# Products of b_o and gates1 between the steps of a recurrence, and a head norm spread over the next job

## The reference

```python
def mlstm_chunkwise(...):                 # branch 1, 4 heads of 128, chunks of 128 tokens
    def step(carry, xs):                  # run forwards and backwards over the 6 chunks
        ...
        w = jnp.exp(dmat - m_t[..., None])
        wqk = w * jnp.einsum('bthd,bshd->bhts', qc, kc)
        num = einsum(wqk, vc) + a[..., None] * einsum(c_prev, qc)
        h = num / jnp.maximum(jnp.abs(den), jnp.exp(-m_t))[..., None]
        ...
        c_new = decay[..., None, None] * c_prev + einsum(ws, vc, kc)
y_b = sigmoid(o_pre) * (h_forward + h_backward)        # o_pre is the product called b_o

def merge_branches(ys, gate_logits, w_branch, w_out):
    g = sigmoid(gate_logits)                           # the products gates0 to gates3
    merged = sum(g[:, :, i] * (y @ w_branch[i]) for i, y in enumerate(ys))
    return merged @ w_out
```

## Time and profile before

| | |
|---|---|
| median of 3 runs | 3787.38 us (3786.98 to 3789.18) |
| the profiled execution, its own time | 3781.9 us |
| its span, first to last instruction | 3780.2 us |
| busy in the span | PE 87%, PEld 78%, DVE 48%, ACT 27%, POOL 11% |
| mean granted TensorE clock | 0.927 of full speed |

### The profile page before, as it was taken

One profiled execution on the slowest core, in us unless ns is written; L12 is line 12 of the kernel. 1 busy time (PEld: TensorE's weight loads), 2 busy tenths in 40 slices (PEclk: granted clock), 3 DMA queues, 4 the chain that ended last, 5 costly groups with the idle time before them and its releaser, 6 DMA issues. The chain is left out here.

```text
span 3780.2 us, 45802 instructions
## 1 busy us (share of the span) xinstructions
PE 3286.8 (87%) x17846; PEld 2934.8 (78%) x17846; DVE 1802.1 (48%) x3302; ACT 1004.6 (27%) x1522; POOL 408.8 (11%) x276
## 2 busy tenths in 40 slices
PE   6977999988999888699999968699879998879997
PEld 5966997887789678599999958577767796658785
DVE  6666135423337674576111375724433376543334
ACT  2211224413221433211211222123423324332221
POOL 0001000010011001222022020100010010111011
PEclk6987999998999999799999979799989999889998
DMA  5500220121124003152221232032121250233332
GB/s 182 162 14 12 56 90 24 62 78 40 34 103 138 23 23 130 73 154 84 72 61 53 82 122 92 1 78 78 38 92 51 67 173 23 77 124 89 94 90 94
DMA packets 328783, 295.82 MB, mean 78 GB/s; under 512 B 39502, under 2 KB 307996, under 8 KB 326812
## 3 DMA queue, kind: packets, MB, share of 16 engines
q1 hardware_dynamic: 315406, 229.74, 20.4%
q10 hardware_dynamic: 13198, 63.65, 4.5%
HBM read 262.54 MB, written 30.41 MB: 77 GB/s over the span
## 5 line engine op out<-in xcount | busy, mean ns | idle before, releaser
L720 PE MATMUL ps<-u_hi,w_hi 128*128 128x384 f32 (+1 forms) x2592 | 759.8, 354 | 69.4 <-ACTq L391 19.1
L720 PE MATMUL ps<-u_lo,w_hi 128*128 128x384 f32 (+1 forms) x2592 | 752.3, 351 | 0.0
L720 PE MATMUL ps<-u_hi,w_lo 128*128 128x384 f32 (+1 forms) x2592 | 751.8, 351 | 0.0
L1407 DVE TENSOR_TENSOR w_lo<-w_raw,w_hi 128x2048 fp32r<-128x2048 f32 x155 | 378.3, 2441 | 582.5 <-ACT w_hi L1080 581.3
L720 PEld LDWEIGHTS ps<-u_hi,w_hi 128*128 128x128 f32 x2592 | 477.0, 191 | 107.3 <-issue 46.1
L720 PEld LDWEIGHTS ps<-u_lo,w_hi 128*128 128x128 f32 x2592 | 479.7, 190 | 25.4
L720 PEld LDWEIGHTS ps<-u_hi,w_lo 128*128 128x128 f32 x2592 | 478.3, 190 | 26.0
L1080 ACT ACTIVATE w_hi<-w_raw 128x2048 fp32r<-128x2048 f32 x155 | 296.4, 1913 | 537.0 <-PE ps L720 297.5
L1108 ACT ACTIVATE space<-ps 128x768 f32<-128x768 f32 (+3 forms) x158 | 117.4, 745 | 702.5 <-PE ps L720 691.0
L882 PE MATMUL ps<-space 128*128 128x128 f32 (+1 forms) x1472 | 209.8, 290 | 72.6 <-DVE space L1680 63.3
L882 PEld LDWEIGHTS ps<-space 128*128 128x128 f32 x1472 | 184.4, 199 | 109.8 <-DVE space L1680 82.5
(11 more groups left out here) (227 smaller groups left out, 4480.0 us busy)
## 6 DMA issues: line engine op xcount, KB each, us to landing
w_raw<-in_w_in SPq DMA_DIRECT2D x288, 256.0 KB, 4.1
space<-in_w_mod SPq DMA_DIRECT2D x48, 1024.0 KB, 5.4
w_raw<-in_w_gate_up SPq DMA_DIRECT2D x176, 256.0 KB, 4.0
w_raw<-in_w_down SPq DMA_DIRECT2D x96, 192.0 KB, 2.8
w_raw<-in_w_branch SPq DMA_DIRECT2D x64, 256.0 KB, 3.6
h_scratch<-space ACTq DMA_DIRECT2D x4, 3072.0 KB, 9.3
space<-h_scratch ACTq DMA_DIRECT2D x4, 3072.0 KB, 10.0
m_scratch<-space ACTq DMA_DIRECT2D x3, 3072.0 KB, 10.8
```

The source lines that it names most:

```text
L720: last = nc.tensor.matmul(ps[:, 2 * (t % 2) + b, 0:a1 - a0], wv[w][:, k, j * P:(j + 1) * P], xx[:, k, a0:a1], start=(k == 0 and w == 0 and ...
L1407: V.tensor_tensor(w_lo[slot][:, :], w_raw[slot][:, :], w_hi[slot][:, :].bitcast(F32), ALU.subtract).then_inc(w_lo_done, 1)
```

## The change

There are four parts.

1. **b_o and most of gates1 move into the recurrence.** The phase `mlstm` gets the 4 tiles of b_o and 6 of the 8 tiles of gates1 (`PARKED1`), worked off in pieces between the parts of a step, with `fill_products` and PSUM bank 2. `mlstm_chunks` says how many chunks of 24 matmuls a step gets: 2, 2, 1 in turn in layer 0 (20 chunks), one in ten of the twelve steps in layer 1. A chunk is cut in three: 12, 8 and 4 matmuls (24, 14 and 10 for two chunks), after `rows`, after the next scores, and after the next keys. The gemm phase of b_o is gone; the gemm phase of gates1 keeps 2 tiles (`gates1_rest`).
2. **The step is rearranged for it.** `products` is cut into `scores` and `keys`; keys now come behind the values and share bank 3 with the transposed weights, so the transposes of the weights also wait for m_kws, DVE's read of the keys. ACT takes the chunks out of PSUM with a plain copy; b_o stays in place and gets its sigmoid at the end of the phase, gates1 tiles go by two staging buffers to DRAM (`g_dram`), come back in `gate_b`, and get their sigmoid in the next phase. c_st moves to make room. Weight units are rounded by ACT and DVE inside the steps.
3. **The head norm of kind d is spread.** Of the two sums of squares, one stays on DVE (`norm_cap`), the other is taken by ACT with four squares that sum as they go (`head_squares`). The small arithmetic (`norm_sums`) and the scaling (`norm_scale`) stand in the next job, POOL takes a second small product, and the block's transposes come one job later (`late = 2`).
4. **Gate products of kinds a and c.** In a job ahead of which no scores are made, half of its gate products stand between the transposes of the job before and its values, instead of behind the values. In all kinds the last job's share moves behind its transposes: a third ahead of the values, the rest behind them.

```diff
-        phases += [("prep_b", l, None), ("mlstm", l, None)]
-        gemm(Group(l, "b_o", 2, 2, KD, q, "u", "sigmoid", 0))
+        phases.append(("prep_b", l, None))
+        phases.append(("mlstm", l, [Group(l, "b_o", 2, 2, KD, q, "u", "fill", 0),
+                                    Group(l, "gates1", PARKED1 // 2, 2, KD, q, "u", "fill", None)]))
         phases.append(("gate_b", l, None))
...
-        gemm(Group(l, "gates1", 4, 2, KD, q, "u", "sigmoid", 20),
+        gemm(Group(l, "gates1_rest", (KD - PARKED1) // 2, 2, KD, q, "u", "sigmoid", 20 + PARKED1),
              Group(l, "branch1", 2, 4, HEADS, q, "y", "merge", (1, 0)))
...
+def mlstm_chunks(l):
+    return [1, 1, 1, 1, 0, 1, 1, 1, 1, 0, 1, 1] if l == DEPTH - 1 else [2, 2, 1] * 4
...
# PE, attention
                 for i in range(len(jobs)):
-                    if (i + 1) % pair == 0 and i + 1 < len(jobs):
+                    final = i + 1 == len(jobs)
+                    scored = (i + 1) % pair == 0 and not final
+                    if scored:
                         scores(i + 1)
+                    elif not final:
+                        fill(fill_quota(l, kind, i) // 2)
                     if i:
                         values(i - 1)
-                    if i > 1 and (i - 1) % heads == 0:
-                        tile_t(i - 2)
-                    for _ in range(fill_quota(l, kind, i)):
-                        next(products)
+                    if i > late and (i - late) % heads == 0:
+                        tile_t(i - late - 1)
+                    if not final:
+                        fill(fill_quota(l, kind, i) - (0 if scored else fill_quota(l, kind, i) // 2))
                     probs_t(i)
+                fill(fill_quota(l, kind, len(jobs) - 1) // 3)
                 values(len(jobs) - 1)
+                fill(fill_quota(l, kind, len(jobs) - 1) - fill_quota(l, kind, len(jobs) - 1) // 3)
                 tile_t(len(jobs) - 1)
...
# PE, recurrence
+                def fill(k, place):
+                    for _ in range({0: (0, 0, 0), 1: (12, 8, 4), 2: (24, 14, 10)}[counts[k]][place]):
+                        next(fills)
...
-                    if k + 1 < len(steps):
+                    if more:
                         rows(k + 1)
+                    fill(k, 0)
                     if want:
                         pe.wait_ge(m_wqk, w + 1)
+                        pe.wait_ge(m_kws, i + 1)
...
-                    if k + 1 < len(steps):
-                        products(k + 1)
+                    if more:
+                        scores(k + 1)
+                    fill(k, 1)
...
+                    if more:
+                        keys(k + 1)
+                    fill(k, 2)
+                    if want:
                         pe.wait_ge(m_num, n.lstm_w)
...
# ACT, kind d
+                def head_squares(q):
+                    act.wait_ge(y_copied, job0 + heads * (q + 1))
+                    ...
+                    for h in range(heads):
+                        last = A(rest, y[:, cols], ACT.Square, scale=2.0 ** -68, accum_out=ssq[:, 1, h:h + 1])
+                    last.then_inc(sq_done, 1)
...
# DVE, kind d
                     if i:
                         finish(i - 1)
-                    if i > 1 and (i - 1) % heads == 0:
-                        yt_low((i - 1) // heads - 1)
+                    if kind == "d" and i > 1 and i % heads == 1:
+                        norm_sums()
+                    if i > late and (i - late) % heads == 0:
+                        yt_low((i - late) // heads - 1)
                     pt_copy(i)
+                    if kind == "d" and i > 1 and i % heads == 1:
+                        norm_scale(i // heads - 1)
```

More of the change, by code:

```diff
@@ L13 @@
 from contextlib import ExitStack
+from itertools import chain
 import numpy as np
@@ L185, in pairs, with mlstm_split_steps @@
         body(i // 2, i % 2)
+def mlstm_chunks(l):
+    return [1, 1, 1, 1, 0, 1, 1, 1, 1, 0, 1, 1] if l == DEPTH - 1 else [2, 2, 1] * 4
+def mlstm_split_steps(l):
+    counts, per = mlstm_chunks(l), 2 * (1 if l == DEPTH - 1 else 2)
+    return [next(k for k in range(2 * NT) if sum(counts[:k + 1]) > per * v) for v in range(2 + PARKED1 // 2)]
 def fill_quota(l, kind, i):
@@ L810, in fill_products @@
                                 for m, (w, xx) in enumerate(((0, x_hi), (0, x_lo), (1, x_hi))):
[L811 removed]
+                                    last = nc.tensor.matmul(ps[:, fill_bank, 0:cols.stop - cols.start],
                                                             wv[w][:, k, j * P:(j + 1) * P], xx[:, k, cols],
@@ L822, in attend, with fill @@
                 pair = 1 if kind == "d" else 2
-                products = fill_products(g)
+                products = fill_products(g, FILL_BANK)
+                def fill(count):
+                    for _ in range(count):
+                        next(products)
                 def scores(i):
@@ L916, in _, with mlstm @@
             n_mixed = [0]
-            def mlstm(l):
-                steps = mlstm_steps(l)
+            def mlstm(l, groups):
+                steps, counts = mlstm_steps(l), mlstm_chunks(l)
+                fills = chain(*(fill_products(g, M_FILL_BANK) for g in groups))
+                def fill(k, place):
+                    for _ in range({0: (0, 0, 0), 1: (12, 8, 4), 2: (24, 14, 10)}[counts[k]][place]):
+                        next(fills)
                 def rows(k):
@@ L928, in rows, with scores @@
                                      stop=True).then_inc(m_rows, 1)
-                def products(k):
+                def scores(k):
                     _, ch, want, _ = steps[k]
@@ L938, in products, with keys @@
                         last.then_inc(m_scores, 1)
+                def keys(k):
+                    _, ch, _, _ = steps[k]
+                    cs = slice(ch * P, (ch + 1) * P)
                     if n.lstm + k:
@@ L941, in products @@
                     for h in range(HEADS):
-                        last = nc.tensor.transpose(ps[:, 2, h * P:(h + 1) * P], space[:, 16 + h, cs], ident[:, :])
+                        last = nc.tensor.transpose(ps[:, 3, h * P:(h + 1) * P], space[:, 16 + h, cs], ident[:, :])
                     last.then_inc(m_keys, 1)
                 rows(0)
-                products(0)
+                scores(0)
+                keys(0)
                 for k, (d, ch, want, _) in enumerate(steps):
@@ L1082, in gemm_unit @@
             def gemm_unit(g, it, s):
+                l = g.layer
                 if not (g.early and isinstance(it, int) and 2 * it + s == 0):
                     split(g, it, s)
+                if g.name == "gates1_rest" and 2 * it + s == 0:
+                    act.wait_ge(g_loaded, 16 * (l + 1))
+                    for tile in range(20, 20 + PARKED1):
+                        A(space[:, tile, toks(g.lat)], space[:, tile, toks(g.lat)], ACT.Sigmoid).then_inc(gate_sig, 1)
                 if g.kind == "merge" and g.dst[0] != 1 and 2 * it + s == 0:
@@ L1259, in attend @@
                 yt0 = n.yt
+                late = 2 if kind == "d" else 1
                 yt_tiles = [jobs[i][0] for i in range(heads - 1, len(jobs), heads)]
@@ L1271, in attend @@
                         exps(i + 1)
-                    if i > 1 and (i - 1) % heads == 0:
+                    if i > late and (i - late) % heads == 0:
                         yt_copy()
+                    while i + 1 < len(jobs) and evicted < fill_done(l, kind, i):
+                        fill_evict(evicted)
+                        evicted += 1
                     pt_copy(i)
@@ L1300, in mlstm @@
                         exps(k + 1)
+                    fill_split(k)
+                    if counts[k]:
+                        fill_evict(evicted)
+                        evicted += 1
+                for tile in range(HEADS):
+                    act.wait_ge(acc_free[0], (t0 + 1 + HEADS * halves) // 2)
+                    act.wait_ge(acc_free[1], (t0 + HEADS * halves) // 2)
+                    A(space[:, tile, toks(groups[0].lat)], space[:, tile, toks(groups[0].lat)],
+                      ACT.Sigmoid).then_inc(o_sig, 1)
                 n.lstm += len(steps)
@@ L1754, in attend, with mlstm, fill_split @@
                 n.yt += len(yt_tiles)
-            def mlstm(l):
+            def mlstm(l, groups):
+                at_steps = mlstm_split_steps(l)
+                def fill_split(k):
+                    for v in (v for v, first in enumerate(at_steps) if first + 1 == k):
+                        u = groups[0].u0 + v + 1
+                        dve.wait_ge(w_hi_done, u + 1)
+                        V.tensor_tensor(w_lo[u % 2][:, :], w_raw[u % 2][:, :], w_hi[u % 2][:, :].bitcast(F32),
+                                        ALU.subtract).then_inc(w_lo_done, 1)
                 def bc(ap, width):
```

141 lines of the change are left out of this document (94 added, 47 removed).

## The result

| | before | changed |
|---|---|---|
| median | 3787.52 us (3786.98 to 3789.18) | 3642.13 us (3641.07 to 3643.3, 4 runs) |
| the profiled execution, its own time | 3781.9 us | 3641.28 us |
| its span | 3780.2 us | 3639.6 us |
| mean granted TensorE clock | 0.927 | 0.937 |

The ratio is 0.9619, with a 95% interval of 0.9604 to 0.9633: the kernel is 145 us faster. Forecast were 98, and 3642 lies outside the range of 3650 to 3738. The direction and the mechanism were right, three sizes were not. In what follows part 1 is points 1 and 2 of the change, part 2 its point 3 and part 3 its point 4, as in the prediction.

What follows compares the result with a forecast made beforehand. TensorE was taken to bound the kernel, except where exchange with VectorE sets the pace. Recurrence products -42, head norm -28 and gate products -28 sum to -98: 3684 us profiled, 3690 as median, range 3650 to 3738.

Steps and rivals of the forecast that it cites:

- the case in which it swings as before: Recurrence: rival that the clock keeps swinging at mean 0.78; gain only 37 us, 3750 us; chance 0.13.
- the slower case: Recurrence: rival that pauses hold the mean clock below 0.70; at 0.5 throughout +142, 3930 us; chance 0.05.
- The stall that takes the place of the old one in kind d: Kind d: transposes of the probabilities wait for y_lo; new stall of 2.5 us, up to 3.5 if POOL is slow.
- the attention edits do nothing: Attention: rival that copies come late by as much as products moved; 15 us instead of 56, 3731 us; chance 0.08.
- the price of a wait in kinds a and c: Values' waits, 35.1 us, about 0.5 each, covered by products, less 0.1 per new start: -28, bounds 0 and -36.
- the walk of a step: Recurrence, layer 0: adding a step's instructions at full clock gave 16.7 us with two chunks, 12.9 with one.
- 198: Recurrence stage of layer 0: forecast length in us, 193 at full clock plus 5 of slow running, against 139.8 before.
- slow running: Recurrence: allowance for time below full clock added to the walk, 5 us in layer 0 and 4 in layer 1.
- The small terms: Around the recurrence: parked gates' return hidden under remaining gates1 products; lower clock into short stages costs 2 us a layer, +4.
- I take -3 in each layer: Kind d's stage end: PE's 7.54 us wait for the norm shrinks, net of POOL's product and lost transpose cover.
- -14.5 and -7.5: Kind d's blocks: forecast gain in us over five blocks in layer 0 and three in layer 1.
- more is gained: Rival: full clock in the recurrence (9 us less), nearly all kind d stall gone (30 less); about -137, 3650; chance 0.17.

Runs made afterwards that it cites:

- e5: Changed kernel without products between a recurrence step's keys and new state, moved to the earlier pieces (12, 12, 0 and 24, 24, 0); 3676.62 us.
- e2: Kernel before with only the spread head norm of kind d added; 3752.02 us, ratio 0.9908.
- e3: Kernel before with only the split of the gate products, the last job's share behind its transposes; 3731.35 us, ratio 0.9854.
- e4: e3 with two gate products between transposes and values in place of half of the job's; 3749.16 us, ratio 0.99.
- e7: Changed kernel; in kind d ACT makes y_hi ahead of the exponentials, DVE makes y_lo behind the mix, ahead of the two maxima; 3626.19 us.

## Why the prediction fell short

**What was right.** b_o and the 6 tiles of gates1 gave back 142.9 us for 141.7. The clock in the recurrence was forecast at 0.9 or more and is 0.95 and 0.94; so the case in which it swings as before is out, and the slower case with it. The Trainium skill, "TensorE: Matmul & The Clock Gate", section "A second HAM failure mode: psum-queue depth-cycling", has the clock swing under frequent micro-idles between groups. The trace agrees for two pauses a step in layer 0 (0.78 in before, 0.90 in e5), not for one (0.95), and not in layer 1 of e5 (0.94 with both). The stall that takes the place of the old one in kind d was forecast at 2.5 us, up to 3.5, ahead of the transposes and for y_lo; it measured 0.9 to 3.1 in layer 0, 2.0 on the mean, and 2.2 in each block of layer 1. That the attention edits do nothing is out too: e2 and e3 give 34 and 55.

**What failed, first: the price of a wait in kinds a and c.** The step was "The 35.1 us of waits of L882 are about 0.5 each", with "The bounds are 0 and -36". The 35.1 are the listed idle time, and e3, e4 and before show that a wait costs PE the idle time and the tail of the instruction ahead of it: 0.75 for a listed 0.52 in the pair above. Of that 0.72 was won, so the 0.1 taken off for a new start was not seen there either. In the four stages 32 us of listed waits went, at 59 places, and 47 us were won, 0.25 more a place than listed; 28 were forecast, and the upper bound was no bound. That is 19 us.

**Second: the walk of a step.** "16.7" and "12.9" were 15.65 and 12.1 (the latter from one L968 to the next, 267.4 to 279.5). Eight and four steps make 8.4 + 3.2 = 11.6 of the 13.5 us by which 198 missed 184.5. The other 1.9 are slow running: two steps took 17.1 and 17.3 us, 3.1 above the rest, where 5 were taken. Of the 11.6 some 3 are a slip in adding: the walk's own terms, 14.2, 1.16, 0.7 and 0.45, give 16.5 and not 16.7, and its terms with one chunk give 12.6 and not 12.9. The rest can be read in the step above, counted from its first row. L1005 starts at 5.85, walked 6.04; from there to L1016 are 3.78, walked 4.0; from L1016 to L1036 3.96, walked 4.2. The products in these pieces were sized right (the 10 ahead of L1036 take 1.82 for 1.8). Too long were the short groups between them, because durations with their tails had been added. L1981 starts at 14.76, walked 15.36; from there to the next diagonal are 0.89, taken as 0.7 + 0.45. All of these errors have one sign, as has that of part 3: listed durations overlap, and a chain that adds them is too long. In layer 1 154 was 147.2. Together 20 us. The small terms, put at +4, came to +2 (`gate_b` is 1.2 and 0.7 longer), and b_o and gates1 gave 1 more.

**Third: kind d.** The end of the stage was mis-sized: "I take -3 in each layer", and the wait there went from 7.54 to 2.48 in layer 0 and from 7.5 to 3.4 in layer 1, -5.1 and -4.1. With the norm alone (e2) it is 5.3 in both layers, -2.2; the other 2.8 and 1.9 are just the cover that the prediction gave the last products. What failed are the two terms that it took off again: 0.5 for POOL's second product, of which 0.20 were seen, and 1.5 for the cover that the last transposes lose, which the wait does not show. That is 3 of the 7 us. The other 4 are in the blocks, -17.4 and -8.8 for "-14.5 and -7.5": the new stall was 2.0 and 2.2 for 2.5, and PE is busy 3.9 and 2.5 us less with the same matmuls, at a clock of 0.95 and 0.93 for 0.90. Which of the two makes the 4 is not shown.

All three erred towards too little, and the low end of the range, 3650, had no room for that: it allowed 9 us in the recurrence, 30 in kind d and none in kinds a and c. The rival "more is gained" so had about the right size for the wrong reasons: kind d gave 7 and not 30, kinds a and c 19, part 1 23.

**Left open.** Why every third step of layer 0 and the steps of layer 1 kept the clock in e5 with both pauses, and how the 4 us of kind d's blocks divide.

## What to carry to other kernels

Price a wait of TensorE from start to start: from the start of the instruction ahead of it to the start of the one that waited, less what the first takes when something follows at once. The listed idle time leaves the tail out, and on short groups of matmuls that was half as much again. It counts only where the work put into the hole can start at once: in kind c of layer 1 that work itself waited for a PSUM bank, and the tail was not won. Where a dependent chain is walked, take each step from start to start too, and look for a place behind the last piece before filling the others more: the one pause left uncovered was worth 16 us a layer. Where a long stall goes, look at the busy time too: in e7 over half of the gain was PE's own, with the same matmuls.

## What the runs showed of the hardware

- The way from the start of four 128x128 transposes, through the copy of their PSUM by ScalarE and VectorE, to the start of the matmuls that read it is 1.11 us; 0.52 of that is listed as idle. Four products of 384 columns fit in (1.14), two do not (1.11 with 0.16 idle).
- With a pause of 1.72 us every 12 to 16 us the recurrence of layer 0 ran at 0.95. With a second one of 1.08 us ahead of it in the step it ran at 0.90, and at two steps of three the first large matmul behind the two took 2.08 us in place of 1.13; with 1.5 to 1.8 us as the second one and no products, before, it ran at 0.78. In layer 1 the same two pauses left 0.94.
- POOL's small power took 1.01 us, and a small product right behind it 0.20.
